# Score products of the low queries on 64 rows, one in each half of the array, in a hybrid attention and convolution layer

## The chip, the cores and the metric

The kernel runs on one core of one Trainium2 chip. The metric is the device time of one execution in microseconds (us); of several runs the median is given.

## The reference

One decoder layer on x of 1024 tokens by 1024 channels, in float32. A normalised x goes through one projection. Half of its columns feed native sparse attention with 8 heads of 64 in 2 groups of 4, the other half a gated convolution of width 3. Both results are gated, joined, projected and added to x. What matters here is the score part. With 16 blocks of 64 tokens and a top-k of 16, every block is selected, so the "selected" branch is plain causal attention:

```python
s_c = einsum('bgqrd,bcgd->bgqrc', qb, k_c) * scale   # 64 compressed blocks
s_s = einsum('bgqrd,bgqnld->bgqrnl', qb, k_g) * scale # selected keys, causal
s_w = einsum('bgqrd,bkgd->bgqrk', qb, k_wb) * scale   # window of 512 keys
p_x = masked_softmax(s_x, mask_x)                     # each branch by itself
o_x = einsum(p_x, v_x)                                # then gated and summed
```

## The kernel before

**Precision.** TensorE multiplies operands of type float32r. To keep more digits, every operand is split in two, high part + low part (hi = the value cast to float32r, lo = value - hi). A product of two split operands over 128 rows takes three matrix products (`three`, L1449 to L1453): hi·hi, hi·lo, lo·hi. A head has only 64 channels, and that is used in the scores: the queries are stored twice, one copy above the other (`qd`, then `qh` and `ql` of 128 rows), and the keys with their high part in rows 0 to 63 and their low part in rows 64 to 127 (`kst`). So qh times kst is hi·hi + hi·lo in one product of 128 rows, and ql times kst is the second (`keys_times`, L1602 to L1605): lo·hi and, with it, lo·lo.

**Tiles and steps.** Queries and keys are cut in 8 tiles of 128 tokens. A unit is a query tile i with a group g, in the order i = 0 to 7, g = 0, 1. Each unit has 8 steps: one of the selected branch for each of its 4 heads, over the keys of tiles 0 to i, then one for each head of window and compressed blocks, over the tiles max(0, i-4) to i and 64 block keys. `scores(k)` (L1607 to L1631) makes the score row of step k in `sc[k % 2]`, which is two PSUM banks of 512 columns. A product stays within one bank, so a row of more than 512 columns is cut in two pieces (`sel_column`, `win_column`, `end_column`: they place the row so that it spans the bank border). A selected row has 2 products up to tile 3 and 4 from tile 4 on. The last window tile stands next to the 64 block keys in a buffer of its own, `kend`, so that both are one product of 192 columns: GpSimd copies the keys of tile i into it once per unit (`copy_last_keys`, L646 to L651).

**The order of a step.** Everything is written out by hand for `STEPS` steps. TensorE in step k: it turns (transposes) a tile of four heads' probabilities of an earlier job (L1761), multiplies the turned tile before it by the values (`flush`, L1738 to L1742), puts in its share of side work (`channels`: input projections of the convolution and gates, later `output`: the output projection, L1451 to L1453), and then makes the score row k+1. VectorE adds the mask and takes the row's maximum (L1358), ScalarE takes the exponential (L936, L940, L942), VectorE, ScalarE and GpSimd scale it by the gate and the reciprocal sum. Turned tiles are cast to a high part by ScalarE (L952), and VectorE forms the low part (L1380). `scores(k)` waits for the exponential of step k-2, which read the same buffer. TensorE gets its weights by a load (LDWEIGHTS, in the profile as PEld) ahead of each product.

**Keys.** In the preparation, before step 0, TensorE turns the keys into `xt`, ScalarE casts all 128 rows to `kst` (L774), and VectorE replaces rows 64 to 127 by the low part (`key_lo`, L1082 to L1084), 512 columns in one instruction, 8 in all. The keys of the compressed blocks are made in the same way and lie in `kend[:, g, 128:192]` (L894, L1280).

Of the kernel before, what the change touches and what calls it, by code (L numbers as in the profile page):

```python
# [7 lines left out]
F32 = mybir.dt.float32  # L8
F32R = mybir.dt.float32r
BF16 = mybir.dt.bfloat16  # L10
U16 = mybir.dt.uint16
ALU = mybir.AluOpType
# [3 lines left out]
P = 128  # L16
# [113 lines left out]
    return [("w", j) for j in range(max(0, i - WT), i + 1)] + [("c", 0)]  # L130


def sel_column(i):

    n = i + 1
    return 0 if n <= 4 else 512 - (n + 1) // 2 * P


def end_column(i):

    return 512 if i >= 3 else i * P


def win_column(i):
    return end_column(i) - min(i, WT) * P


def turns_at(k):
# [72 lines left out]

WIDE_STEP = next(k for k in range(NS) if k // 4 % 2 and end_column(UNITS[k // 8][0]) == 512)
EARLY = (SIDE_AT[2 * (WIDE_STEP - 2)]) // 8


# [91 lines left out]
def hybrid_layer(nc: bass.Bass, x, xcm, wpack, wside, wout, normw, qnorm, knorm, par, const, maskc, out):  # L319
    with ExitStack() as ctx:  # L320
# [5 lines left out]
        gate = sb("gate", [P, NT, 3 * HEADS])  # L326
        kend = sb("kend", [P, GROUPS, P + CB], F32R)
        vcmp = sb("vcmp", [P, GROUPS, P], F32R)
        nmax = sb("nmax", [P, 4, 2])
        psums = sb("psums", [P, 4, 2])  # L330
        precip = sb("precip", [P, 4, 2])
# [103 lines left out]
        wor_in = [sem(f"wor_in{s}") for s in range(4)]  # L435
        woh_ready, wol_ready = sem("woh_ready"), sem("wol_ready")
        qd_ready, qh_ready, kend_ready = sem("qd_ready"), sem("qh_ready"), sem("kend_ready")
        s_done, max_ready, exp_done = sem("s_done"), sem("max_ready"), sem("exp_done")
        recip_ready, factor_ready = sem("recip_ready"), sem("factor_ready")
        p_act, p_dve, cmp_scaled = sem("p_act"), sem("p_dve"), sem("cmp_scaled")  # L440
# [167 lines left out]
        def _(pool):  # L608
# [57 lines left out]
            for k in range(STEPS):  # L666
                s = k - 1
                if 0 <= s < NS and s // 4 % 2 == 1:
                    i, _ = UNITS[s // 8]
                    pool.wait_ge(recip_ready, s + 1)  # L670
                    p = cmp_probs(i, s % 4)
                    nc.gpsimd.tensor_scalar(p, p, precip[:, s % 4, 1:2], gate_of(s, 0), ALU.mult, ALU.mult)\  # L672
                        .then_inc(cmp_scaled, 1)
                u = unit_at(k, -5)
                if u:
                    copy_queries(u)
                u = unit_at(k, -6)
                if u is not None and u >= 2:
                    copy_last_keys(u)
                for h in halves_at(k):  # L680
                    half_lo(h)
                for j in wout_at(k):
                    kt, cols = wout_piece(j)
                    pool.wait_ge(woh_ready, j + 1)
                    nc.gpsimd.tensor_tensor(wol[:, kt, cols], weight_rows(j)[:, :], woh[:, kt, cols].bitcast(F32), ALU.subtract)\
                        .then_inc(wol_ready, 1)
                m = mixn_half_at(k)
                if m is not None:
                    pool.wait_ge(msh_ready, 2 * m + 2)
                    nc.gpsimd.tensor_tensor(msl[:, 0:4, :], mixn[:, :, m * P:(m + 1) * P],  # L690
                                            msh[:, 0:4, :].bitcast(F32), ALU.subtract).then_inc(msl_ready, 1)
                m = mixc_half_at(k)
                if m is not None:
                    pool.wait_ge(msh_ready, 2 * m + 1)
                    nc.gpsimd.tensor_tensor(msl[:, 4:8, :], mixc[:, :, m * P:(m + 1) * P],
                                            msh[:, 4:8, :].bitcast(F32), ALU.subtract).then_inc(msl_ready, 1)
# [3 lines left out]
        def _(act):  # L700
# [227 lines left out]
            def exponentials(s):  # L928
                w, h = divmod(s, 4)
                i, g = UNITS[w // 2]  # L930
                act.wait_ge(max_ready, s + 1)
                if h == 0 and w >= 2:
                    act.wait_ge(tp_done, tp_end[w - 2])
                if w % 2 == 0:
                    o = sel_column(i)
                    A(sel_probs(i, h), sc[s % 2][:, o:o + (i + 1) * P], ACT.Exp, scale=-1.0,  # L936
                      bias=nmax[:, s % 4, 0:1], accum_out=psums[:, s % 4, 0:1]).then_inc(exp_done, 1)
                else:
                    e = end_column(i)
                    A(cmp_probs(i, h), sc[s % 2][:, e + P:e + P + CB], ACT.Exp, scale=-1.0,  # L940
                      bias=nmax[:, s % 4, 1:2], accum_out=psums[:, s % 4, 1:2])
                    A(win_probs(i, h), sc[s % 2][:, win_column(i):e + P], ACT.Exp, scale=-1.0,  # L942
                      bias=nmax[:, s % 4, 0:1], accum_out=psums[:, s % 4, 0:1]).then_inc(exp_done, 1)

            def prob_hi(kind):
# [12 lines left out]
            for k in range(STEPS):  # L958
                _, turned = turns_at(k)
                if 1 <= k <= NS:  # L960
                    exponentials(k - 1)
                for kind, _ in turned[:1]:
                    prob_hi(kind)
                if k - 1 in CONV_STEPS:
# [50 lines left out]
        def _(dve):  # L1015
# [64 lines left out]
                        .then_inc(dve_rel, 1)  # L1080

            def key_lo(n, dst):  # L1082
                dve.wait_ge(kt_hi, n + 1)
                V.tensor_tensor(dst, xt[n % 2][HD:P, :], dst.bitcast(F32), ALU.subtract).then_inc(kt_ready, 1)  # L1084

            def channel_lo(k):

# [115 lines left out]
            def keys_lo(first, n0, b):  # L1203

                for n in (first, first + 1):
                    key_lo(n0 + n, kst[HD:P, b, n // 2, (n % 2) * 512:(n % 2 + 1) * 512])

            def positions(f):

# [150 lines left out]
            def maxima(s):  # L1360
                w, _ = divmod(s, 4)
                i, g = UNITS[w // 2]
                dve.wait_ge(s_done, s + 1)
                if w % 2 == 0:
                    o = sel_column(i)
                    masked_maxima(sc[s % 2][:, o:o + (i + 1) * P], causal(i + 1), nmax[:, s % 4, 0:1]).then_inc(max_ready, 1)
                else:
                    e = end_column(i)
                    masked_maxima(sc[s % 2][:, e + P:e + P + CB], blocked[:, i, :], nmax[:, s % 4, 1:2])
                    masked_maxima(sc[s % 2][:, win_column(i):e + P], banded if i >= WT else causal(i + 1),  # L1370
                                  nmax[:, s % 4, 0:1]).then_inc(max_ready, 1)

            def prob_lo(kind):
# [72 lines left out]
        def _(pe):  # L1446
# [155 lines left out]
            def keys_times(dst, keys, h):  # L1602

                MM(dst, qh[:, h, :], keys, start=True, stop=False)  # L1604
                return MM(dst, ql[:, h, :], keys, start=False, stop=True)  # L1605

            def scores(k):  # L1607
                w, h = divmod(k, 4)
                i, g = UNITS[w // 2]
                if h == 0 and w % 2 == 0:  # L1610
                    pe.wait_ge(tp_read, q_tp[w // 2])
                if h == 0 and w % 2 == 1:
                    pe.wait_ge(kend_ready, w // 2 + 1)
                if k >= 2:
                    pe.wait_ge(exp_done, k - 1)
                if k == WIDE_STEP:
                    bank_free(pe, EARLY - 1)
                    bank_free(pe, EARLY - 2)
                s = sc[k % 2]
                if w % 2 == 0:  # L1620
                    o, n = sel_column(i), i + 1
                    first = min(n, 4 - o // P)
                    for a, b in ((0, first), (first, n)):
                        if a < b:
                            ins = keys_times(s[:, o + a * P:o + b * P], kst[:, 0, g, a * P:b * P], h)
                else:
                    o, e, j0 = win_column(i), end_column(i), max(0, i - WT)
                    if j0 < i:
                        keys_times(s[:, o:e], kst[:, 1, g, j0 * P:i * P], h)
                    ins = keys_times(s[:, e:e + P + CB], kend[:, g, :], h)  # L1630
                ins.then_inc(s_done, 1)  # L1631

            def channels(p):
# [112 lines left out]
            def turn(n, kind, j):  # L1746

                nonlocal tpn, ptn, pending
                i, g = UNITS[n // 2]
                if tpn >= 2:  # L1750
                    pe.wait_ge(tp_read, tpn - 1)
                r = CB if kind == "c" else P
                for h in range(GH):
                    if kind == "s":
                        src = sel_probs(i, h)[:, j * P:(j + 1) * P]
                    elif kind == "w":
                        c = j - max(0, i - WT)
                        src = win_probs(i, h)[:, c * P:(c + 1) * P]
                    else:
                        src = cmp_probs(i, h)  # L1760
                    ins = nc.tensor.transpose(tp[tpn % 2][0:r, h * P:(h + 1) * P], src, ident)  # L1761
                ins.then_inc(tp_done, 1)
                tpn += 1
                tp_of[ptn] = tpn
                flush()
                pending = (n, (kind, j), ptn, n % 2 == 0 and j == 0)
                ptn += 1
# [42 lines left out]
def mask_constants():  # L1810
# [2 lines left out]
    r, k = np.arange(P)[:, None], np.arange(P)[None, :]  # L1813
    near = np.where(k <= r, 0, NEG)
    m[:, B_SEL + SEQ - P:B_SEL + SEQ] = near
    m[:, B_WIN:B_WIN + P] = np.where(k > r, 0, NEG)
    m[:, B_CMP - P:B_CMP] = near
    for i in range(NT):
        o = B_CMP + i * CB
# [29 lines left out]
```

## Time and profile before

| | us |
|---|---|
| median of 3 runs (lowest, highest) | 665.57 (665.19, 665.87) |
| the profiled execution, its own time | 665.02 |
| its span in the trace | 663.2 |
| TensorE matmul busy | 653.1 |
| TensorE weight loads busy | 551.7 |
| VectorE busy | 487.0 |
| ScalarE busy | 377.7 |
| GpSimd busy | 200.8 |

The span is cut off at the first and last instruction, so the profiled execution is 1.8 us longer than it. The granted TensorE clock is 1.00 of full speed in the whole span, which is 2.4 GHz. In a timeline row the length of a product runs from its start to its modelled end; products overlap, so their rate is read from one start to the next. "x4" is four like instructions in one row. "128\*128" is rows times columns of the array in use.

### The profile page before, as it was taken

Reading aid. Unit: us, or ns where it says so; the run is one execution under the profiler, and the core shown is the slowest. Engines: PE = TensorE matmul, PEld = TensorE weight load, DVE = VectorE, ACT = ScalarE, POOL = GpSimd, SP = SyncE. Lnnn points to the kernel's source line nnn. Section 1 sums busy time; section 2 is a strip of 40 time slices with the busy share of each in tenths; the row PEclk is TensorE's granted clock in tenths of the full one; section 3 lists DMA queues with packets and bytes.
Section 4 is the critical chain, followed back from the end, with each engine's and each line's share of the span. In section 5 each row is a group of like instructions: output and inputs, shape, how many; then the busy total and the mean of one; then the engine's idle time right before and its main releaser. Section 6 shows DMA issues by size and latency. Waiting matters only on the chain.

```text
span 663.2 us, 10318 instructions
## 1 busy us (share of the span) xinstructions
PE 653.1 (98%) x3513; PEld 551.7 (83%) x3513; DVE 487.0 (73%) x1152; ACT 377.7 (57%) x872; POOL 200.8 (30%) x220
## 2 busy tenths in 40 slices
PE   9999999999999999999999999998999999999998
PEld 6889998888888888888888888886878888888886
DVE  5956989986747655775797876888887778787853
ACT  6754458554435444555565665767775655555651
POOL 3433304433423232321312312158532221211210
PEclk9999999999999999999999999999999999999999
DMA  8413202202111111101101100143111011011101
GB/s 316 150 56 113 64 1 65 64 17 64 47 49 33 36 44 33 39 26 33 33 16 33 33 17 26 39 127 127 64 48 50 32 49 48 32 45 39 45 33 64
DMA packets 20212, 37.35 MB, mean 56 GB/s; under 512 B 2880, under 2 KB 4288, under 8 KB 20160
## 3 DMA queue, kind: packets, MB, share of 16 engines
q1 hardware_dynamic: 20016, 36.68, 17.2%
q8 instruction: 29, 0.48, 0.3%
q14 instruction: 23, 0.19, 0.1%
q10 hardware_dynamic: 144, 0.00, 0.0%
HBM read 32.48 MB, written 4.19 MB: 55 GB/s over the span
## 4 chain that ended last, share of the span: by engine, by line
PE 87%; DVE 9%; ACT 2%; issue 1%; ACTq 0%; DVEq 0%
PE pf L1451 10%; PE pf L1452 10%; PE pf L1453 10%; PE tp L1761 8%; PE sc L1605 5%; PE sc L1604 4%; PE po L1741 4%; PE po L1742 4%; PE pj L1453 4%; PE pj L1452 4%; PE pj L1451 4%; PE sc L1451 3%; PE sc L1453 3%; PE sc L1452 3%; DVE sc L1358 2%
## 5 line engine op out<-in xcount | busy, mean ns | idle before, releaser
L952 ACT CAST pth<-tp 128x512 fp32r<-128x512 f32 (+1 forms) x148 | 86.8, 587 | 122.4 <-PE tp L1761 121.8
L1358 DVE CUSTOM_DVE_ANT_0 sc<-sc,maskb 128x64 f32<-128x64 f32 (+8 forms) x192 | 103.1, 561 | 47.2 <-PE sc L1605 46.3
L1380 DVE TENSOR_TENSOR ptl<-tp,pth 128x512 fp32r<-128x512 f32 x132 | 91.0, 690 | 30.5 <-ACT pth L952 30.2
L672 POOL TENSOR_SCALAR qp<-qp,precip,gate 128x64 f32<-128x64 f32 x64 | 41.4, 647 | 192.6 <-DVE precip L1348 192.4
L1761 PE MATMUL tp<-cst,qp 128*128 128x128 f32 (+1 forms) x592 | 88.9, 273 | 0.5 <-issue 0.2
L632 POOL TENSOR_TENSOR fl<-fraw,fh 128x512 fp32r<-128x512 f32 x40 | 54.1, 1352 | 101.4 <-ACT fh L797 101.4
L1451 PE MATMUL pf<-hh,fh 128*128 128x512 f32 x200 | 80.4, 402 | 2.3 <-DVE th L1318 1.6
L1452 PE MATMUL pf<-hl,fh 128*128 128x512 f32 x200 | 78.4, 392 | 0.0
L1453 PE MATMUL pf<-hh,fl 128*128 128x512 f32 x200 | 78.1, 391 | 0.0
L1761 PEld LDWEIGHTS tp<-cst,qp 128*128 128x128 f32 (+1 forms) x592 | 68.6, 137 | 11.2 <-issue 1.5
L623 POOL TENSOR_TENSOR wl<-qp,wh 128x512 fp32r<-128x512 f32 (+1 forms) x33 | 49.3, 1516 | 87.4 <-ACT wh L712 83.8
L1741 PE MATMUL po<-pth,val 128*128 128x512 f32 x132 | 62.6, 474 | 2.4 <-DVE ptl L1380 1.7
L1354 DVE TENSOR_SCALAR qp<-qp,precip,gate 128x640 f32<-128x640 f32 (+7 forms) x96 | 59.2, 616 | 3.6
L936 ACT ACTIVATE qp<-sc,nmax 128x128 f32<-128x128 f32 (+7 forms) x64 | 47.5, 743 | 8.3 <-DVE nmax L1358 8.2
L1605 PE MATMUL sc<-kst,ql 128*128 128x512 f32 (+3 forms) x152 | 52.2, 346 | 0.0
L1742 PE MATMUL po<-ptl,val 128*128 128x512 f32 x132 | 51.9, 394 | 0.0
L1604 PE MATMUL sc<-kst,qh 128*128 128x512 f32 (+3 forms) x152 | 51.5, 339 | 0.0
L1451 PE MATMUL pf<-woh,msh 128*128 128x512 f32 x120 | 47.7, 398 | 0.2 <-DVE xo L1389 0.2
L1451 PEld LDWEIGHTS pf<-hh,fh 128*128 128x128 f32 x200 | 37.6, 188 | 11.9 <-DVE th L1318 3.0
L1452 PE MATMUL pf<-wol,msh 128*128 128x512 f32 x120 | 47.5, 396 | 0.0
L1453 PE MATMUL pf<-woh,msl 128*128 128x512 f32 x120 | 47.4, 395 | 0.0
L1453 PEld LDWEIGHTS pf<-hh,fl 128*128 128x128 f32 x200 | 37.6, 188 | 8.6
(256 smaller groups left out, 1556.2 us busy)
## 6 DMA issues: line engine op xcount, KB each, us to landing
fraw<-in_wside SPq DMA_DIRECT2D x40, 256.0 KB, 2.6
qp<-in_wpack SPq DMA_DIRECT2D x28, 256.0 KB, 3.1
xo<-in_x SPq DMA_DIRECT2D x16, 256.0 KB, 2.5
out<-xo SPq DMA_DIRECT2D x16, 256.0 KB, 2.1
wor<-in_wout SPq DMA_DIRECT2D x12, 256.0 KB, 2.8
mixc<-in_xcm SPq DMA_DIRECT2D x4, 512.0 KB, 7.1
xlow<-in_xcm SPq DMA_DIRECT2D x3, 512.0 KB, 5.9
qp<-in_wpack SPq DMA_DIRECT2D x5, 224.0 KB, 2.6
```

Source lines behind the costliest of these rows:

```text
L952: nc.scalar.copy(pth[ptn % 2][0:r, :], tp[tpn % 2][0:r, :]).then_inc(pth_ready, 1)
L1354: V.tensor_scalar(p, p, factor, main, ALU.mult, ALU.mult).then_inc(p_dve, 1)
L1358: return V.tensor_tensor_reduce(row, row, mask, -1.0, -NEG, ALU.add, ALU.min, most)
L1380: V.tensor_tensor(ptl[ptn % 2][:, :], tp[tpn % 2][:, :], pth[ptn % 2][:, :].bitcast(F32), ALU.subtract).then_inc(tp_read, 1)
L1451: MM(dst, lh, rh, start=start, stop=False)
L1452: MM(dst, lh, rl, start=False, stop=False)
L1453: return MM(dst, ll, rh, start=False, stop=stop)
L1604: MM(dst, qh[:, h, :], keys, start=True, stop=False)
L1605: return MM(dst, ql[:, h, :], keys, start=False, stop=True)
L1741: MM(po[:, :], v, pth[pt % 2][:, :], start=first, stop=False)
L1742: MM(po[:, :], v, ptl[pt % 2][:, :], start=False, stop=False).then_inc(pv_done, 1)
L1761: ins = nc.tensor.transpose(tp[tpn % 2][0:r, h * P:(h + 1) * P], src, ident)
```

## The change

It puts key tiles in two classes by the parity of their number. A tile of the query tile's own parity is an "own" tile, the rest are "other" tiles.

- Keys of odd tiles are stored with the parts exchanged: low part in rows 0 to 63, high part in rows 64 to 127. So `key_lo` writes two pieces of 64 rows by 256 columns, one for each parity, where it wrote one of 64 by 512.
- From query tile 4 (selected) and 3 (window) on, a score row is laid out as other tiles, then own tiles, with the bank border between them. The order of the tiles in a row is followed when probabilities are turned, and the mask of the oldest window tile moves to its new place.
- There a new function, `by_row_groups`, makes the row: the products with `qh` keep 128 rows, one per bank; the products with `ql` have 64 rows, those of the high key parts alone, so the own and the other tiles' products stand in different halves of the array and write different banks. The lo·lo term goes.
- The 64 block keys become a product of their own (high and low queries), next to the other tiles. They need a copy with the parts exchanged, `kcs`, for even query tiles: ScalarE makes it once, in step 3, by two copies of 64 rows by 128 columns.
- From tile 3 on, GpSimd no longer copies the last keys (10 of 16 copies go).

```diff
+def sel_split(i):
+    return i >= 4
+def win_split(i):
+    return i >= 3
+def sel_order(i):
+    own, other = range(i % 2, i + 1, 2), range(1 - i % 2, i + 1, 2)
+    return [*other, *own] if sel_split(i) else list(range(i + 1))
+def win_order(i):
+    tiles = range(max(0, i - WT), i + 1)
+    return sorted(tiles, key=lambda j: j % 2 == i % 2) if win_split(i) else list(tiles)
 def sel_column(i):
-    n = i + 1
-    return 0 if n <= 4 else 512 - (n + 1) // 2 * P
-def end_column(i):
-    return 512 if i >= 3 else i * P
+    return 512 - (i + 1) // 2 * P if sel_split(i) else 0
 def win_column(i):
-    return end_column(i) - min(i, WT) * P
+    return 512 - 2 * P if win_split(i) else 0
+def cmp_column(i):
+    return win_column(i) - CB if win_split(i) else (i + 1) * P
...
+                if k == KCS_STEP:
+                    act.wait_ge(kt_ready, 9)
+                    nc.scalar.copy(kcs[HD:P, :, :], kend[0:HD, :, P:P + CB])
+                    nc.scalar.copy(kcs[0:HD, :, :], kend[HD:P, :, P:P + CB]).then_inc(kcs_ready, 1)
...
             def key_lo(n, dst):
                 dve.wait_ge(kt_hi, n + 1)
-                V.tensor_tensor(dst, xt[n % 2][HD:P, :], dst.bitcast(F32), ALU.subtract).then_inc(kt_ready, 1)
+                for odd in range(2):
+                    rows = slice(0, HD) if odd else slice(HD, P)
+                    low = dst[rows, :].rearrange("p (t u c) -> p u t c", u=2, c=P)[:, odd]
+                    both = xt[n % 2][rows, :].rearrange("p (t u c) -> p u t c", u=2, c=P)[:, odd]
+                    ins = V.tensor_tensor(low, both, low.bitcast(F32), ALU.subtract)
+                ins.then_inc(kt_ready, 1)
...
+            def by_row_groups(row, b, g, i, j0, h, with_blocks):
+                def tiles(parity):
+                    js = range(j0 + (parity - j0) % 2, i + 1, 2)
+                    return len(js) * P, kst[:, b, g, :].rearrange("p (t u c) -> p u t c", u=2, c=P)[:, parity, js[0] // 2:js[-1] // 2 + 1, :]
+                def span(lo, hi):
+                    return row[:, lo:hi].rearrange("p (t c) -> p t c", c=P)
+                own, other = i % 2, 1 - i % 2
+                hi_rows = [slice(0, HD), slice(HD, P)]
+                n_own, k_own = tiles(own)
+                n_other, k_other = tiles(other)
+                to_own, to_other = span(512, 512 + n_own), span(512 - n_other, 512)
+                c = 512 - n_other - CB
+                to_cmp, k_cmp = row[:, c:c + CB], kcs[:, g, :] if other else kend[:, g, P:P + CB]
+                MM(to_other, qh[:, h, :], k_other, start=True, stop=False)
+                if with_blocks:
+                    MM(to_cmp, qh[:, h, :], k_cmp, start=False, stop=False, skip_group_check=True)
+                MM(to_own, qh[:, h, :], k_own, start=True, stop=False)
+                MM(to_own, ql[hi_rows[own], h, :], k_own[hi_rows[own]], start=False, stop=True)
+                ins = MM(to_other, ql[hi_rows[other], h, :], k_other[hi_rows[other]], start=False, stop=True)
+                if with_blocks:
+                    ins = MM(to_cmp, ql[hi_rows[other], h, :], k_cmp[hi_rows[other]], start=False, stop=True, skip_group_check=True)
+                return ins
...
                 if w % 2 == 0:
-                    o, n = sel_column(i), i + 1
-                    first = min(n, 4 - o // P)
-                    for a, b in ((0, first), (first, n)):
-                        if a < b:
-                            ins = keys_times(s[:, o + a * P:o + b * P], kst[:, 0, g, a * P:b * P], h)
+                    if sel_split(i):
+                        ins = by_row_groups(s, 0, g, i, 0, h, False)
+                    else:
+                        ins = keys_times(s[:, 0:(i + 1) * P], kst[:, 0, g, 0:(i + 1) * P], h)
+                elif win_split(i):
+                    ins = by_row_groups(s, 1, g, i, max(0, i - WT), h, True)
                 else:
-                    o, e, j0 = win_column(i), end_column(i), max(0, i - WT)
-                    if j0 < i:
-                        keys_times(s[:, o:e], kst[:, 1, g, j0 * P:i * P], h)
-                    ins = keys_times(s[:, e:e + P + CB], kend[:, g, :], h)
+                    if i:
+                        keys_times(s[:, 0:i * P], kst[:, 1, g, 0:i * P], h)
+                    ins = keys_times(s[:, i * P:(i + 1) * P + CB], kend[:, g, :], h)
```

## Rows read from the trace of the kernel before

**Rows 1.** The page: TensorE's busy time; engines' shares of the chain
```profile
PE 653.1 (98%) x3513; PEld 551.7 (83%) x3513; DVE 487.0 (73%) x1152; ACT 377.7 (57%) x872; POOL 200.8 (30%) x220
...
PE 87%; DVE 9%; ACT 2%; issue 1%; ACTq 0%; DVEq 0%
```

**Rows 2.** Waits of TensorE: us in total, times, longest
```profile
PE po L1741 <- DVE ptl L1380: 1.7, 3, 1.2
```

**Rows 3.** Timeline of TensorE, selected step of tile 4: start, length
```profile
403.15 0.34 PE L1604 MATMUL sc<-kst,qh 128*128 128x384 f32 x1
403.33 0.34 PE L1605 MATMUL sc<-kst,ql 128*128 128x384 f32 x1
403.50 0.28 PE L1604 MATMUL sc<-kst,qh 128*128 128x256 f32 x1
403.62 0.28 PE L1605 MATMUL sc<-kst,ql 128*128 128x256 f32 x1
403.74 0.60 PE L1761 MATMUL tp<-cst,qp 128*128 128x128 f32 x4
```

**Rows 4.** The same, tile 6 selected: first product, and what follows
```profile
503.19 0.39 PE L1604 MATMUL sc<-kst,qh 128*128 128x512 f32 x1
...
504.00 0.60 PE L1761 MATMUL tp<-cst,qp 128*128 128x128 f32 x4
```

**Rows 5.** The same, tile 7 selected: first product, and what follows
```profile
566.01 0.39 PE L1604 MATMUL sc<-kst,qh 128*128 128x512 f32 x1
...
566.92 0.60 PE L1761 MATMUL tp<-cst,qp 128*128 128x128 f32 x4
```

**Rows 6.** The same, a window step of tile 7
```profile
560.51 0.40 PE L1604 MATMUL sc<-kst,qh 128*128 128x512 f32 x1
560.75 0.39 PE L1605 MATMUL sc<-kst,ql 128*128 128x512 f32 x1
560.98 0.25 PE L1604 MATMUL sc<-kend,qh 128*128 128x192 f32 x1
561.07 0.28 PE L1605 MATMUL sc<-kend,ql 128*128 128x192 f32 x1
561.18 0.60 PE L1596 MATMUL tp<-cst,qd 128*128 128x128 f32 x4
```

**Rows 7.** The same, tile 3 window: first product, and what follows
```profile
360.72 0.34 PE L1604 MATMUL sc<-kst,qh 128*128 128x384 f32 x1
...
361.27 0.60 PE L1761 MATMUL tp<-cst,qp 128*128 128x128 f32 x4
```

**Rows 8.** Timeline of TensorE's weight loads near the step of rows 5
```profile
566.01 0.19 PEld L1605 LDWEIGHTS sc<-kst,ql 128*128 128x128 f32 x1
...
567.25 0.19 PEld L1741 LDWEIGHTS po<-pth,val 128*128 128x128 f32 x1
567.36 0.19 PEld L1742 LDWEIGHTS po<-ptl,val 128*128 128x128 f32 x1
```

**Rows 9.** Timeline of TensorE, a turn of 64-column weights between others
```profile
422.18 0.39 PE L1453 MATMUL pf<-hh,fl 128*128 128x512 f32 x1
422.41 0.60 PE L1761 MATMUL tp<-cst,qp 128*64 128x128 f32 x4
422.77 0.48 PE L1741 MATMUL po<-pth,val 128*128 128x512 f32 x1
```

**Rows 10.** Low parts of keys, L1084 and L1280: ns min/median/max
```profile
L1084 DVE TENSOR_TENSOR kst<-xt,kst x8: 686/692/695, 109.3 to 153.5; 64x512 fp32r<-64x512 f32 x8
...
L1280 DVE TENSOR_TENSOR kend<-xt,kend x1: 295/295/295, 155.2 to 155.2; 64x128 fp32r<-64x128 f32 x1
```

**Rows 11.** Timeline, end of the preparation: VectorE, TensorE's wait
```profile
152.92 1.30 DVE L1084 TENSOR_TENSOR kst<-xt,kst 64x512 fp32r<-64x512 f32 x2 [0.18 <-ACT kst L774]
...
153.76 0.30 PE L1708 MATMUL xt<-cst,ckr 128*128 128x128 f32 x1 [0.18 <-DVE kst L1084]
```

**Rows 12.** Busy us of the stretch: PE, PEld, DVE, ACT, POOL
```profile
440.00:510.00 70.00, 67.33 (x361) 55.72 (x359) 57.62 (x129) 48.94 (x109) 37.41 (x39) 1.00 0.25 86
```

More of the change, by code:

```diff
@@ L220, in halves_at @@
     return out
-WIDE_STEP = next(k for k in range(NS) if k // 4 % 2 and end_column(UNITS[k // 8][0]) == 512)
+WIDE_STEP = next(k for k in range(NS) if k // 4 % 2 and win_split(UNITS[k // 8][0]))
+KCS_STEP = 3
 EARLY = (SIDE_AT[2 * (WIDE_STEP - 2)]) // 8
@@ L328, in hybrid_layer @@
         vcmp = sb("vcmp", [P, GROUPS, P], F32R)
+        kcs = sb("kcs", [P, GROUPS, CB], F32R)
         nmax = sb("nmax", [P, 4, 2])
@@ L437, in hybrid_layer @@
         qd_ready, qh_ready, kend_ready = sem("qd_ready"), sem("qh_ready"), sem("kend_ready")
+        kcs_ready = sem("kcs_ready")
         s_done, max_ready, exp_done = sem("s_done"), sem("max_ready"), sem("exp_done")
@@ L677, in _ @@
                 u = unit_at(k, -6)
-                if u is not None and u >= 2:
+                if u is not None and u >= 2 and not win_split(UNITS[u][0]):
                     copy_last_keys(u)
@@ L938, in exponentials @@
                 else:
-                    e = end_column(i)
-                    A(cmp_probs(i, h), sc[s % 2][:, e + P:e + P + CB], ACT.Exp, scale=-1.0,
+                    c, o = cmp_column(i), win_column(i)
+                    A(cmp_probs(i, h), sc[s % 2][:, c:c + CB], ACT.Exp, scale=-1.0,
                       bias=nmax[:, s % 4, 1:2], accum_out=psums[:, s % 4, 1:2])
-                    A(win_probs(i, h), sc[s % 2][:, win_column(i):e + P], ACT.Exp, scale=-1.0,
+                    A(win_probs(i, h), sc[s % 2][:, o:o + (min(i, WT) + 1) * P], ACT.Exp, scale=-1.0,
                       bias=nmax[:, s % 4, 0:1], accum_out=psums[:, s % 4, 0:1]).then_inc(exp_done, 1)
@@ L1205, in keys_lo @@
                 for n in (first, first + 1):
-                    key_lo(n0 + n, kst[HD:P, b, n // 2, (n % 2) * 512:(n % 2 + 1) * 512])
+                    key_lo(n0 + n, kst[:, b, n // 2, (n % 2) * 512:(n % 2 + 1) * 512])
             def positions(f):
@@ L1367, in maxima @@
                 else:
-                    e = end_column(i)
-                    masked_maxima(sc[s % 2][:, e + P:e + P + CB], blocked[:, i, :], nmax[:, s % 4, 1:2])
-                    masked_maxima(sc[s % 2][:, win_column(i):e + P], banded if i >= WT else causal(i + 1),
+                    c, o = cmp_column(i), win_column(i)
+                    masked_maxima(sc[s % 2][:, c:c + CB], blocked[:, i, :], nmax[:, s % 4, 1:2])
+                    masked_maxima(sc[s % 2][:, o:o + (min(i, WT) + 1) * P], banded if i >= WT else causal(i + 1),
                                   nmax[:, s % 4, 0:1]).then_inc(max_ready, 1)
@@ L1611, in scores @@
                     pe.wait_ge(tp_read, q_tp[w // 2])
-                if h == 0 and w % 2 == 1:
+                if h == 0 and w % 2 == 1 and not win_split(i):
                     pe.wait_ge(kend_ready, w // 2 + 1)
+                if h == 0 and w % 2 == 1 and win_split(i):
+                    pe.wait_ge(kcs_ready, 1)
                 if k >= 2:
@@ L1754, in turn @@
                     if kind == "s":
-                        src = sel_probs(i, h)[:, j * P:(j + 1) * P]
+                        c = sel_order(i).index(j)
+                        src = sel_probs(i, h)[:, c * P:(c + 1) * P]
                     elif kind == "w":
-                        c = j - max(0, i - WT)
+                        c = win_order(i).index(j)
                         src = win_probs(i, h)[:, c * P:(c + 1) * P]
@@ L1815, in mask_constants @@
     m[:, B_SEL + SEQ - P:B_SEL + SEQ] = near
-    m[:, B_WIN:B_WIN + P] = np.where(k > r, 0, NEG)
+    m[:, B_WIN + 2 * P:B_WIN + 3 * P] = np.where(k > r, 0, NEG)
     m[:, B_CMP - P:B_CMP] = near
```

## The prediction, made before the changed kernel was run

> **What bounds the kernel now.** I read the page first: TensorE is busy for 653.1 of 663.2 us, and the chain that ended last lies on it for 87% [rows 1]. A busy TensorE need not be at its rate, so I read the waits next: its largest one, on VectorE's low parts of turned probabilities, is 1.7 us in all [rows 2]. Then the timeline, from one start to the next. Products of 512, 384 and 256 columns follow each other at 0.23, 0.175 and 0.12 us [rows 3 to 5]. The granted clock is 1.00 (2.4 GHz), where 512 columns are 0.213 us, so nearly all of this is streaming. Two products of 192 columns take 0.20 us together, where streaming would be 0.16 [rows 6]: something else sets the pace of short ones. The weight loads show it. The load for a product starts as the product before it starts, and two loads that have nothing to wait for start 0.11 us apart [rows 8]. So a product costs its columns or a load, whichever is longer, and the kernel ends when TensorE has worked through its stream. What a score row costs on TensorE goes into the end one for one, as long as the others keep up.
>
> **Steps before.** From the first product of a step to what follows it: selected rows of tiles 4, 6 and 7 take 0.59, 0.81 and 0.91 us [rows 3 to 5], and tile 5, four products of 384 columns, 4 x 0.175 = 0.70. A window row is 2 x 0.23 + 0.20 = 0.66 from tile 4 on (0.67 for tile 7 [rows 6]) and 0.55 at tile 3 [rows 7]. Each tile has 8 steps of either kind (2 groups x 4 heads), so the change touches 32 selected and 40 window steps.
>
> **Steps after.** The high products stay as they are. The gain is that the two low products, in two halves of the array and on two banks, can run at the same time; the price is two short products for the block keys, a load each. Nothing in this trace runs two products at once, so I bound it. I count from the start of the own tiles' high product. *Value taken:* loads go one after another, 0.11 us apart as now [rows 8], but the load of the second half need not wait for the first half's product, since it fills another half. It is then ready at 0.22.
> - Tile 4: 0.12 (other, high) + 0.175 (own, high) + 0.175 (own, low); the other low one runs from 0.22 to 0.34 and is hidden: 0.47, saves 0.12.
> - Tile 5: 0.175 + (0.22 + 0.175) = 0.57, saves 0.13.
> - Tile 6: 0.175 + 0.23 + 0.23 = 0.635, saves 0.175.
> - Tile 7: 0.23 + 0.23 + 0.23 = 0.69, saves 0.22.
> - Together 0.645 us, times 8: **5.2 us off**.
> - Window: 0.12 (other, high) + 0.11 (blocks, high, a load), then other low from 0.22 to 0.34, the blocks' low product at 0.34 and only then the load of what follows, ready at 0.45: 0.68. That is 0.02 more than 0.66 in 32 steps (0.6 us) and 0.13 more than 0.55 in 8 (1.0 us): **1.6 us on**.
>
> Net 3.6 us off. *Upper bound:* the two halves' loads run together, so the other low product starts with the own one. Then tile 5 saves 0.17 and the rest stay (0.685 x 8 = 5.5), a window step is 0.64 from tile 4 on (0.6 us off) and 0.58 at tile 3 (0.2 us on): 5.9 us off. I take the first, since single loads 0.11 us apart are what rows show.
>
> The Trainium skill ("TensorE: Matmul & The Clock Gate", The mechanism) says that products in different row groups start about 4 ns apart, their loads overlapping. No run here shows that yet; by it the sum would be the upper bound, 5.9.
>
> **The other edits.** `key_lo`: 512 columns take 0.692 us, 128 take 0.295 [rows 10], so 0.163 + 0.00103 per column, and 256 take 0.43. Two like instructions overlap by 0.08 (1.30 for two [rows 11]). So a piece costs 2 x 0.35 instead of 0.61, 0.08 more. At the end of the preparation VectorE is what TensorE waits for (0.18 us on L1708 [rows 11]), and three pieces lie before that point: 0.25 us on, at least 0 and, with nothing overlapped, 3 x 0.16 = 0.5. ScalarE's two copies for `kcs` come in step 3, with waits all long fulfilled; the nearest row, 64 x 128 on VectorE, is 0.3 us [rows 10]. ScalarE is 57% busy [rows 1], and TensorE needs `kcs` only at tile 3, so nothing; the same for GpSimd's ten copies that go. VectorE and ScalarE read rows of the same length as before. They must do it in less time, though: where they are most busy, VectorE has 57.6 of 70 us [rows 12], and TensorE's time in such a stretch falls by about 1%. The waits of TensorE for L1380 and its like may grow a little: 0.3 us on, bounds 0 and 1.
>
> **Sum.** 3.6 - 0.25 - 0.3 = 3.0 us off. Against the profiled execution, 665.02, that gives 662.0; it lies 0.55 under the median of the runs, 665.57, so the median comes to **662.5**. About 0.2%, 1.3 us, is what a measurement of this kernel can tell from no change.
>
> **Rivals.**
> 1. *The array must run empty between full and half use (slower).* Each changed step goes from 128 rows to 64 and back, 144 changes. A product of 512 columns is in flight for 0.39 us where the next starts after 0.23 [rows 5, 8]: the overhang of 0.16 us would be exposed each time, 144 x 0.16 = 23 us on, 685.5 in all; if the load can't run ahead either, 144 x 0.11 = 16 more, about 701. If only a part of the pipe must be empty it decides from 3.0 / 144 = 0.021 us a change; at 0.1 it gives 677. Against it: the kernel already alternates between full products and turns with 64-column weights, and there the first of four 64-column turns starts 0.23 after a full product, and a full one follows 0.36 after it, which three loads at 0.11 explain [rows 8, 9]. That is a change of columns, though, in transposes, and not of rows. For it: nothing in the trace but that no row-wise change was seen. The Trainium skill ("TensorEngine Tiling (Array Packing)", Key Properties) says that changing the tiling mode drains TensorE. Rows 9 don't show such a drain for columns; by that rule the time is this rival's. Chance 0.30.
> 2. *The halves don't overlap (or the product of 64 rows is run as one of the whole array).* Then the change doesn't do what it says: selected steps cost the same, window steps 0.12 + 0.11 + 0.175 + 0.175 + 0.12 + 0.11 = 0.81 (0.15 on, 32 times), at tile 3 0.70 (0.15 on, 8 times): 6.0 us on, with the smaller terms 6.6, so 672.1. For it: rows show products strictly one after another. Against it: they all claim the same rows. Chance 0.13.
> 3. *The overlap works, but the second half's load waits for the first half's low product to start*, as each load now waits for the product before it [rows 8]. The other low product is then 0.11 late: the selected steps save 0.065, 0.065, 0.12 and 0.11 (2.9 us), window steps lose 0.085 and 0.14 (3.8 us): 0.9 on, 1.5 with the smaller terms, so 667.0. Against it: that order has its reason in one spare place for weights, which the second half has free. Chance 0.11.
>
> **How the numbers follow.** The forecast, with the upper bound, has 0.46; by itself its range is 659.3 to 664.3. The range over all must reach into rival 1: up to a price of 0.1 us a change, 677, which takes in rivals 2 and 3. The full drain lies above it, with 0.15, and little is under 659.3. Faster by over 0.2%: the forecast less its weak end, 0.45 (with a drain under 0.01 us, 0.46). Within 0.2%: that weak end, a drain of about 0.02, half of rival 3: 0.12. Slower: the rest, 0.42.
>
> **What the profile would show.** Right: the own and the other low product of a step start at most some 0.05 us apart (0.01 for the upper bound), the step of tile 7 takes 0.69 from first product to next work, and window steps are near 0.68. A gap of over 0.02 us between the own high product's streaming and the own low one's start, and the same on return, would be rival 1; low products 0.23 apart at tile 7, rival 2; 0.11 apart, rival 3. Outside the score rows TensorE's starts should be unchanged, and the waits of L1741 on L1380 should not grow by more than 1 us. I would be wrong altogether if VectorE took over as the releaser of TensorE in most steps of tiles 6 and 7.

## The result and the profile after

The changed kernel takes **679.00 us** (678.53 to 679.17, 5 runs) against 665.57 before (665.19 to 665.87): 1.0199 times as long, with a 95% interval of 1.0188 to 1.021. It is slower by 13.4 us, where 662.5 and a range of 659.3 to 677.0 were forecast.

The page of the changed kernel, its busy times and the chain that ended last:

```profile
PE 666.7 (98%) x3593; PEld 547.6 (81%) x3593; DVE 491.6 (73%) x1160; ACT 378.8 (56%) x874; POOL 200.0 (30%) x210
...
PE 87%; DVE 9%; ACT 2%; issue 1%; DMA 1%; SPq 0%; ACTq 0%; DVEq 0%
```

The shares are those of [rows 1]; the kernel is still bound by TensorE, which has 80 products more (two short ones in each of 40 window steps). Its waits, in us in total, times and longest:

```profile
PE po L1800 <- DVE ptl L1411: 1.9, 4, 1.2
PE xt L1767 <- DVE kst L1114: 1.2, 1, 1.2
...
PE pf L1482 <- DVE th L1349: 0.8, 1, 0.8
```

The wait on turned probabilities is as it was [rows 2]. The second is the wait at the end of the preparation, 0.18 us before [rows 11]. So nearly all of the 13.4 us is in TensorE's own stream. The same step as in [rows 5], the selected row of tile 7, in its timeline (start us, length us):

```profile
576.91 0.39 PE L1654 MATMUL sc<-kst,qh 128*128 128x512 f32 x1
577.13 0.40 PE L1657 MATMUL sc<-kst,qh 128*128 128x512 f32 x1
577.46 0.50 PE L1658 MATMUL sc<-kst,ql 64*128 64x512 f32 x1
577.46 0.49 PE L1659 MATMUL sc<-kst,ql 64*128 64x512 f32 x1
577.89 0.65 PE L1821 MATMUL tp<-cst,qp 128*128 128x128 f32 x4
578.30 0.48 PE L1800 MATMUL po<-pth,val 128*128 128x512 f32 x1
```

and the weight loads of the same stretch:

```profile
577.46 0.18 PEld L1658 LDWEIGHTS sc<-kst,ql 64*128 64x128 f32 x1 [0.36 <-issue]
577.46 0.18 PEld L1659 LDWEIGHTS sc<-kst,ql 64*128 64x128 f32 x1
577.89 0.42 PEld L1821 LDWEIGHTS tp<-cst,qp 128*128 128x128 f32 x4 [0.24 <-issue]
```

I call the products of 64 rows the half mode, and a run of them between two products of the whole array a visit to it. Two things are to be seen. The overlap works, and better than I took it: the two low products of 512 columns start together, and so do their loads. But they start 0.33 us after the high product, not 0.23, and their loads start only then, at 577.46, not at 577.13 as the load of a whole-array product does [rows 8]. I read the 0.10 by which they come late as the time in which the array runs empty (the drain), and the 0.11 by which the products last longer, 0.50 instead of 0.39, as the wait for their weights. On the way back it is the same: 0.43 to the turn (0.11 for the load, 0.21 for the columns, 0.10 late), whose own load starts with it, and 0.41 for the four turns where 0.36 is usual. **By this reading a visit costs 0.10 + 0.11 on the way in and 0.10 + 0.05 on the way out, before a turn.** The step takes 0.98 us plus those 0.05, against 0.91.

To compare all steps I take, for each score row, the time from the end of the product before it to the end of the second one after it, the median of the 8 rows of a kind, and its difference to before. For the window steps of tiles 4 to 7 there is one mean. The columns are the changed kernel and three of the experiments below. The last line adds up every single step, not the medians.

| step | changed | low products whole | one half, no overlap | four changes |
|---|---|---|---|---|
| selected, tile 4 | +0.23 | 0.00 | +0.34 | +0.73 |
| selected, tile 5 | +0.17 | 0.00 | +0.34 | +0.73 |
| selected, tile 6 | +0.17 | 0.00 | +0.345 | +0.74 |
| selected, tile 7 | +0.12 | 0.00 | +0.355 | +0.75 |
| window, tile 3 | +0.30 | +0.11 | +0.32 | +0.72 |
| window, tiles 4 to 7 | +0.255 | +0.11 | +0.32 | +0.72 |
| sum over all steps, us | +15.6 | +4.4 | +23.1 | +51.5 |

Tiles 0 to 2 (and the selected row of tile 3), which the change doesn't split, differ by 0.002 at most. With 1.6 us of the preparation (below) the steps would make 17.2 us, 3.8 more than measured. A part of that can be found: I take TensorE's starts outside the score rows, from the first score row on, and call one late when it comes more than 0.1 us behind the median for the same pair of products. Late starts add up to 10.2 us before (29 of them) and 7.8 after (24). That a slower TensorE finds more of the others' work done fits this, but no run tests it, and the other 1.4 us are open. In the runs below too, steps and preparation together come to 1 to 6 us more than was measured.

### The profile page after: what moved, and what is told of

Read it like the earlier page. It is cut to its first block, busy times and chain, and to the rows that moved or that the text cites. A ratio compares the mean times of both kernels' runs of the same rounds, so it can differ in the third digit from the quotient of the medians.

```text
span 677.0 us, 10478 instructions
## 1 busy us (share of the span) xinstructions
PE 666.7 (98%) x3593; PEld 547.6 (81%) x3593; DVE 491.6 (73%) x1160; ACT 378.8 (56%) x874; POOL 200.0 (30%) x210
## 3 DMA queue, kind: packets, MB, share of 16 engines
q1 hardware_dynamic: 20016, 36.68, 17.2%
## 4 chain that ended last, share of the span: by engine, by line
PE 87%; DVE 9%; ACT 2%; issue 1%; DMA 1%; SPq 0%; ACTq 0%; DVEq 0%
PE pf L1482 10%; PE pf L1483 10%; PE pf L1484 10%; PE tp L1821 10%; PE po L1800 4%; PE po L1801 4%; PE sc L1658 3%; PE sc L1482 3%; PE pj L1483 3%; PE pj L1484 3%; PE pj L1482 3%; PE sc L1484 3%; PE sc L1483 3%; PE sc L1657 2%; PE sc L1654 1%; PE sc L1636 1%
## 5 line engine op out<-in xcount | busy, mean ns | idle before, releaser
L693 POOL TENSOR_SCALAR qp<-qp,precip,gate 128x64 f32<-128x64 f32 x64 | 43.7, 684 | 201.5 <-DVE precip L1379 201.3
L1821 PE MATMUL tp<-cst,qp 128*128 128x128 f32 (+1 forms) x592 | 92.4, 278 | 0.2
L1821 PEld LDWEIGHTS tp<-cst,qp 128*128 128x128 f32 (+1 forms) x592 | 66.4, 137 | 17.1 <-issue 7.5
L1483 PEld LDWEIGHTS pf<-hl,fh 128*128 128x128 f32 x200 | 37.6, 188 | 7.2
L963 ACT ACTIVATE qp<-sc,nmax 128x640 f32<-128x640 f32 (+4 forms) x64 | 42.3, 661 | 0.0
```

Of the source, the lines that this page charges most:

```text
L1483: MM(dst, lh, rl, start=False, stop=False)
```

## The experiments

The theory after the result (A): the overlap works, but each visit of the array to the half mode and back costs about 0.35 us. Its rivals: the layout (B), two products at once (C), a price once a step whatever lies in it (D).

### The low products on the whole array

```diff
-                MM(to_own, ql[hi_rows[own], h, :], k_own[hi_rows[own]], start=False, stop=True)
+                MM(to_own, ql[:, h, :], k_own, start=False, stop=True)
```

and the same for the other tiles and the block keys.

> The changed kernel, with the low queries' products on all 128 rows: same layout, same order and number of products, no half of the array used alone. Theory A (each time the array goes from whole to half use and back costs about 0.35 us, and the overlap itself works): the selected steps go back to their old length (0.91 us at tile 7), window steps stay about 0.15 longer than before in 40 steps (6 us), the preparation stays 1.5 to 2 us later: about 672 us (670.5 to 673.5), 7 under the changed kernel. Theory B (the time is lost in the layout: keys read in strides of two tiles, rows ordered other then own, the exchanged keys): stays at 678 to 680.

Measured: 670.39 us (669.38 to 670.73) against 665.81, ratio 1.0066 (1.0051 to 1.0081); 8.6 under the changed kernel, and 0.1 under the lower end of A's forecast. The selected steps are back at their old length (table), so layout, strided keys and order of the row cost nothing in the rows: B falls. What is left are the preparation and the window steps. One of these, of tile 6 (its block keys come from `kcs`, which even tiles use; the step of [rows 6] is one of tile 6 as well, not of tile 7, whose window steps are as long):

```profile
565.02 0.28 PE L1654 MATMUL sc<-kst,qh 128*128 128x256 f32 x1
565.14 0.19 PE L1656 MATMUL sc<-kcs,qh 128*128 128x64 f32 x1
565.17 0.42 PE L1657 MATMUL sc<-kst,qh 128*128 128x384 f32 x1
565.42 0.34 PE L1658 MATMUL sc<-kst,ql 128*128 128x384 f32 x1
565.60 0.28 PE L1659 MATMUL sc<-kst,ql 128*128 128x256 f32 x1
565.72 0.20 PE L1661 MATMUL sc<-kcs,ql 128*128 128x64 f32 x1
565.75 0.64 PE L1627 MATMUL tp<-cst,qd 128*128 128x128 f32 x4
```

From the first product to the turns it takes 0.73 us, where the row of [rows 6] took 0.67. The 64 block columns are short, 0.03 us to the next start, and it is the product behind each that waits for its load (0.42 instead of 0.34, and the turns 0.64 instead of 0.60). With these 0.05 in the turns, two separate short products cost 0.11 a step, 4.4 us in all.

### One half alone, one product after another

The kernel before, with the two high products first and then both low ones on rows 0 to 63:

```diff
+                for dst, keys in pieces:
+                    MM(dst, qh[:, h, :], keys, start=True, stop=False)
+                for dst, keys in pieces:
+                    ins = MM(dst, ql[0:HD, h, :], keys[0:HD], start=False, stop=True)
```

> The kernel before, with the low queries' products of tiles 4 on (selected) and 3 on (window) made on rows 0 to 63 alone, behind the two high ones, one after another in the same half: 72 visits to the half mode, nothing overlaps. The low.low term is left out in these rows. Theory A: the price of 0.35 us a visit comes without any gain: 72 x 0.35 = 25 us, less some 4 that other waits absorb: about 687 us (683 to 691). Theory C (the price belongs to two products at once, their loads or banks getting in each other's way): 665 to 667.

Measured: 684.74 us (684.5 to 685.31) against 665.81, ratio 1.0285 (1.027 to 1.03). That is 18.9 on, 2 under the middle of A's forecast and inside its bounds; C falls, since nothing runs at once here. A selected step of tile 7:

```profile
580.41 0.62 PE L1610 MATMUL sc<-kst,qh 128*128 128x512 f32 x2
580.97 0.73 PE L1612 MATMUL sc<-kst,ql 64*128 64x512 f32 x2
581.63 0.66 PE L1776 MATMUL tp<-cst,qp 128*128 128x128 f32 x4
582.04 0.48 PE L1756 MATMUL po<-pth,val 128*128 128x512 f32 x1
```

Its loads:

```profile
580.96 0.29 PEld L1612 LDWEIGHTS sc<-kst,ql 64*128 64x128 f32 x2 [0.36 <-issue]
581.62 0.42 PEld L1776 LDWEIGHTS tp<-cst,qp 128*128 128x128 f32 x4 [0.37 <-issue]
```

Two high products take 0.56 to the next start instead of 0.46, and the loads start with what they belong to, at 580.96 and 581.62. Between the two low products, in the same mode, nothing is lost: 0.66 for both, of which 0.11 is the first load and 0.10 the way out. So the price is one of changing, 0.32 to 0.355 us a visit in the table, and hardly depends on the number of columns.

### The control: the same order on the whole array

```diff
-                    ins = MM(dst, ql[0:HD, h, :], keys[0:HD], start=False, stop=True)
+                    ins = MM(dst, ql[:, h, :], keys, start=False, stop=True)
```

> The control of the run before: the same order, both high products and then both low ones, all on 128 rows. Both theories: like the kernel before, 665 to 666.5 us; if the order by itself cost something, it would show here.

Measured: 665.91 us (665.55 to 666.16) against 665.81, ratio 1.0002 (0.9992 to 1.0011). The order costs nothing.

### Four changes a step

The changed kernel with each low product right behind its high one:

```diff
                 MM(to_other, qh[:, h, :], k_other, start=True, stop=False)
+                MM(to_other, ql[hi_rows[other], h, :], k_other[hi_rows[other]], start=False, stop=True)
                 MM(to_own, qh[:, h, :], k_own, start=True, stop=False)
                 MM(to_own, ql[hi_rows[own], h, :], k_own[hi_rows[own]], start=False, stop=True)
-                ins = MM(to_other, ql[hi_rows[other], h, :], k_other[hi_rows[other]], start=False, stop=True)
```

(with the block keys' two products beside those of the other tiles).

> The changed kernel with its products in the order other high, other low, own high, own low: no overlap, and four changes between whole and half in a step instead of two. Theory A: a second price of 0.35 a step and the overlap lost: selected steps 8 x (4 x 0.7) = 22 us over before, window steps 40 x 0.8 = 32, preparation 1.5, less some 5 absorbed: about 716 us (705 to 722). Theory D (the price is paid once a step, by the first use of a half or by the step's end, whatever lies between): the overlap lost alone, about 6 to 9 us over the changed kernel, 685 to 688.

Measured: 712.59 us (712.2 to 712.7) against 665.81, ratio 1.07 (1.0682 to 1.0718). The step of tile 7:

```profile
602.13 0.40 PE L1654 MATMUL sc<-kst,qh 128*128 128x512 f32 x1
602.46 0.50 PE L1657 MATMUL sc<-kst,ql 64*128 64x512 f32 x1
602.89 0.50 PE L1660 MATMUL sc<-kst,qh 128*128 128x512 f32 x1
603.32 0.50 PE L1661 MATMUL sc<-kst,ql 64*128 64x512 f32 x1
603.75 0.65 PE L1820 MATMUL tp<-cst,qp 128*128 128x128 f32 x4
```

The load of the second high product, which is one of the whole array, starts with it as well:

```profile
602.89 0.19 PEld L1660 LDWEIGHTS sc<-kst,qh 128*128 128x128 f32 x1 [0.25 <-issue]
```

Each start comes 0.33 or 0.43 after the one before, 0.43 where that one had to wait for its own load. Two visits cost 0.73 to 0.75 us without the block keys, a little over twice the one visit of the run with one half (0.34 to 0.355), and D falls. The little more is the way out of the first visit: it leads to a product of 512 columns on the whole array, which lasts 0.50 like those of 64 rows, so there the whole 0.11 of the load is exposed, and not 0.05 as before a turn.

### The preparation: key_lo in two pieces

```diff
-                V.tensor_tensor(dst, xt[n % 2][HD:P, :], dst.bitcast(F32), ALU.subtract).then_inc(kt_ready, 1)
+                for odd in range(2):
+                    low = dst.rearrange("p (t u c) -> p u t c", u=2, c=P)[:, odd]
+                    both = xt[n % 2][HD:P, :].rearrange("p (t u c) -> p u t c", u=2, c=P)[:, odd]
+                    ins = V.tensor_tensor(low, both, low.bitcast(F32), ALU.subtract)
+                ins.then_inc(kt_ready, 1)
```

> The kernel before, with key_lo in two pieces of 64 rows by 256 columns (even tiles, odd tiles), both on rows 64 to 127: nothing else changed. If the longer VectorE work in the preparation moves the end: eight instructions become sixteen, 0.225 us more for each pair (four pieces took 1.75 us in the changed kernel, two whole ones 1.30), some seven of them ahead of the last wait: 666.7 to 667.7 us. If the preparation has slack, or the later start of the score steps in the changed kernel's trace is only how that execution began: 665.4 to 666.3.

Measured: 666.22 us (665.91 to 666.94) against 665.43, ratio 1.0012 (1.0004 to 1.0021): 0.8 on. That is under the 666.7 to 667.7 that I expected if the longer work moves the end, and inside the range that I gave for a preparation with slack; the interval is clear of no change, though. The next run says why it is less.

### The preparation: odd tiles' parts exchanged, nothing else

The kernel before with `key_lo` of the changed kernel.

> The kernel before, with the keys of odd tiles stored with their parts exchanged and nothing else (no split rows, no products of 64 rows). The same time as the run with key_lo in two pieces, 666.7 to 667.7 us, if the number of pieces is the cost; more than that, up to 2 us over before, if writing to the other half of the partitions costs something of its own.

Measured: 666.99 us (666.31 to 667.6) against 665.43, ratio 1.0024 (1.0014 to 1.0033): 1.6 on. The last four pieces and TensorE's wait for them, first with both kinds of pieces on rows 64 to 127:

```profile
153.98 1.45 DVE L1087 TENSOR_TENSOR kst<-xt,kst 64x256 fp32r<-64x256 f32 x4 [0.18 <-ACT kst L774]
...
154.89 0.30 PE L1712 MATMUL xt<-cst,ckr 128*128 128x128 f32 x1 [0.55 <-DVE kst L1087]
```

and with the parts exchanged:

```profile
154.07 1.75 DVE L1089 TENSOR_TENSOR kst<-xt,kst 64x256 fp32r<-64x256 f32 x4 [0.18 <-ACT kst L774]
...
155.07 0.30 PE L1714 MATMUL xt<-cst,ckr 128*128 128x128 f32 x1 [1.17 <-DVE kst L1089]
```

Four pieces on the same rows take 1.45 us, 0.15 over the 1.30 of two whole ones [rows 11]: 0.08 for each whole one, as I had worked out. With the pieces alternating between rows 0 to 63 and 64 to 127 they take 1.75, that is 4 x 0.44: they no longer overlap. That is 0.225 for each whole one, of which the alternation is the larger part, 0.15, and the number 0.075. (The 1.6 us lies inside the range that I gave if the number is the cost, but the run before, with the same number of pieces, took 0.8 less, so it isn't the number alone.)

### A longer visit, and its twin on the whole array

The selected rows alone are split, and every low product there is made three times within one visit:

```diff
-                MM(to_own, ql[hi_rows[own], h, :], k_own[hi_rows[own]], start=False, stop=True)
-                ins = MM(to_other, ql[hi_rows[other], h, :], k_other[hi_rows[other]], start=False, stop=True)
+                for r in range(3):
+                    MM(to_own, ql[hi_rows[own], h, :], k_own[hi_rows[own]], start=False, stop=r == 2)
+                    ins = MM(to_other, ql[hi_rows[other], h, :], k_other[hi_rows[other]], start=False, stop=r == 2)
```

> Selected rows split as in the changed kernel, window rows as before, and each low product of a selected split step is made three times (own, other, own, other, own, other) within one visit to the halves, so that a visit hides three times as much; the output counts the low part three times. To be read against its twin on the whole array. Theory A (a visit costs 0.345 us once, the overlap saves 0.12, 0.17, 0.175 and 0.22 us a pass at tiles 4 to 7): 8 x (4 x 0.345 - 3 x 0.685) = 5.4 us under the twin, about 683 us. If a part of the price came with each product of 64 rows instead: over the twin.

The twin has `ql[:, h, :]` and the keys' 128 rows in both.

> The twin: the same three passes of low products on all 128 rows, nothing overlaps, the output again counts the low part three times. Two passes more than one cost 8 x (0.59 + 0.70 + 0.81 + 0.91) = 24 us, the preparation 1.6, less some 3 that waits absorb: about 688.5 us (686 to 690).

Measured: 683.07 us (682.82 to 683.8) in the halves, ratio 1.0264 (1.0249 to 1.028) to before, against 689.17 (688.87 to 689.5) on the whole array, ratio 1.0357 (1.0343 to 1.0372). Here the half mode wins, by 6.1 us. A selected step of tile 7 in the halves:

```profile
585.12 0.40 PE L1660 MATMUL sc<-kst,qh 128*128 128x512 f32 x1
585.45 0.50 PE L1662 MATMUL sc<-kst,ql 64*128 64x512 f32 x1
585.45 0.50 PE L1663 MATMUL sc<-kst,ql 64*128 64x512 f32 x1
585.78 0.39 PE L1662 MATMUL sc<-kst,ql 64*128 64x512 f32 x1
585.79 0.39 PE L1663 MATMUL sc<-kst,ql 64*128 64x512 f32 x1
586.02 0.39 PE L1662 MATMUL sc<-kst,ql 64*128 64x512 f32 x1
586.02 0.39 PE L1663 MATMUL sc<-kst,ql 64*128 64x512 f32 x1
586.34 0.66 PE L1826 MATMUL tp<-cst,qp 128*128 128x128 f32 x4
```

The second pair starts 0.33 after the first (0.11 for the load, then the columns), the third 0.23 after the second: one price per visit, and each pair of 512 columns costs what one product does. Between the twins the step differs by 0.32 us at tile 7 and 0.19 at tiles 5 and 6; at tile 4 they are equal within 0.01. By theory A that is 3 x 0.22, 3 x 0.17 and 3 x 0.12 less 0.345, or 0.32, 0.17 to 0.18, and 0.02.

### The selected rows alone

The changed kernel with `win_split` false and the window row as before.

> The changed kernel with the selected rows alone split (tiles 4 to 7, 32 visits), window and block rows as before, keys stored exchanged. Theory A, from steps of 0.12 to 0.23 us more in the changed kernel's trace (5.3 us), 1.6 for the preparation, less some 1.5 that waits absorb: 671 us (670 to 672). So no part of the change pays by itself. If the selected rows gained and the window rows were all of the loss: under 666.

Measured: 670.85 us (670.23 to 671.19) against 665.40, ratio 1.008 (1.0064 to 1.0097). The selected steps are longer by 0.23, 0.17, 0.17 and 0.12 as in the changed kernel. So no tile pays, not even the one with most to hide.

## Why the prediction was wrong

**The step that failed is the price of changing between whole and half use of the array, which I took as nothing.** It stood as rival 1, with a chance of 0.30. Against it I held that turns with 64-column weights come and go without a gap [rows 9]. They do, but they are transposes with fewer weight columns, and that says nothing of rows. Nor does the trace say that the array changes its mode for them at all: its "128\*64" is only the number of rows and columns in use. The Trainium skill ("TensorEngine Tiling (Array Packing)", Key Properties) says that changing the tiling mode drains TensorE. For a change of rows this case's trace agrees, at about 0.10 us each way; rows 9, which I read as evidence against, don't test it.

**Its size.** I bounded the price by the whole overhang, 0.16, and put the load that can't run ahead, 0.11, only into the far case; the range ended at 0.1 a change. Measured are 0.345 a visit or 0.17 a change: the drain is shorter than the overhang, but the load is exposed as well, fully on the way in and by half on the way out, where a turn follows. That the 0.16 of rival 1 lies near 0.17 is luck: it stood for the drain alone. 72 visits at about 0.33 are 24 us, and put in the place of nothing they take my sum to 686.5. The 7.5 us down to 679.0 are 4.8 by which the steps came out shorter than this (15.6 us on instead of 24 - 3.6 = 20.4; the overlap, below), 3.8 that didn't reach the end, and 1.05 the other way in the smaller terms. (The lower end of the forecast's own range, 659.3, isn't added up from terms either: 5.9 off with nothing for the smaller ones gives 659.7.)

**The overlap** was at my upper bound. In the selected steps the difference between one half without overlap and the changed kernel is 0.11, 0.17, 0.17 and 0.23 us at tiles 4 to 7. That is my upper bound (0.12, 0.17, 0.175, 0.22), not the value taken (0.12, 0.13, 0.175, 0.22), since the two halves' loads run together. In the window steps of tiles 4 to 7 it hid 0.175 us (0.32 for the visit and 0.11 for the separate products, less the 0.255 measured). That again is my upper bound (0.81 - 0.64 = 0.17) and not the value taken (0.81 - 0.68 = 0.13), for the block keys' low product runs beside the own tiles' one too (in one step of tile 6 they start at 571.88 and 571.65, and the turns at 572.03). The Trainium skill ("TensorE: Matmul & The Clock Gate", The mechanism) has products in different row groups start some 4 ns apart; the trace agrees, with both starts at 577.46. Rival 3, a load that waits for the other half's product, was wrong, and so was rival 2.

**The window steps**: without overlap I had 0.15 over before; the whole-array run shows 0.11. I took 0.11 for each of the two short products. The high one costs that, 0.03 to the next start and 0.08 by which the product behind it is late; the low one, before the turns, costs 0.03 + 0.05.

**The smaller terms.** `key_lo`: 0.25 forecast, 1.6 measured. The price of a piece was right for pieces on the same rows; that pieces cost more when they alternate between the halves of the partitions was in no row I read. It also reaches further back than the three pieces that I counted. From the first low part of the keys to the wait of TensorE in [rows 11] it is 44.50 us before (109.26 to 153.76) and 45.93 with the parts exchanged (109.14 to 155.07), 1.43 more. Of that, 0.44 lies between the first two groups of calls, 0.83 between the last two and 0.16 behind; the 31.63 us between the second and the third group are the same in both. The waits of TensorE were to grow by 0.3; the late starts shrank instead. The copies of ScalarE and GpSimd cost nothing that shows, as forecast.

No version that was run beats the kernel before. A visit must hide more than 0.345 us, some 830 columns at 2.4 GHz. The most that a row offers is 512. Two heads' rows in one visit would offer 1024 at tile 7, 0.45 - 0.345 = 0.1 us for each pair, 4 pairs and some 0.4 us in all, against 1.6 for the exchanged keys. I haven't tried that, nor more rows in a visit, which would need more score buffers than the two of `sc`.

## What to carry to other kernels

Products of 64 rows in both halves of the array do run at once, at no cost within a visit, but going there and back costs about as much as 830 columns of streaming. Count visits before columns: collect the half-array work so that one visit hides well over that, or leave it on the whole array. Products with fewer weight columns that come without a gap are no evidence for products with fewer rows.

## What the runs showed of the hardware that I had not expected

- The weights of a product in the other mode aren't loaded while the last product of the old mode runs. The load starts with the product that needs it, 0.33 us after the start of a high product of 512 columns, so 0.11 us of load is exposed on top of a drain of 0.10. The way back to a whole-array product of 512 columns costs the same (the run with four changes), before a turn only 0.05 of the load is exposed. Within a mode, whole or half, loads run ahead.
- Two loads into the two halves start together and take no longer than one: both low products of 512 columns then last 0.50 us, as the first low product of a single half does.
- Instructions of VectorE on 64 partitions and 256 columns follow each other at 0.44 us when they alternate between the two halves of the partitions (1.75 for four), and at 0.34 when they stay in one (1.45 for four); a single one lasts 0.42 to 0.43 in both.
- Open: what a product of float32r with 64 weight columns costs between full ones (only transposes show such weights here, and not whether they change the mode), and how the price divides between drain and load beyond what the starts in the rows show.
